# Squares of a differential head: from one full-precision pass to rounded highs and GpSimd-made lows

## What is computed

```
def rms_norm_2(x, g, eps=1e-6):
    xf = x.astype(jnp.float32)
    y = xf * lax.rsqrt(jnp.mean(xf * xf, axis=-1, keepdims=True) + eps)
    return (y * g.astype(jnp.float32)).astype(x.dtype)
...
    q = rms_norm_2(q.reshape(B, S, H, 2, d), qn_g)
    k = rms_norm_2(k.reshape(B, S, H, 2, d), kn_g)
...
        s = jnp.einsum("bhmqd,bhmkd->bhmqk", qblk, kt).astype(jnp.float32) * scale
...
        p = jax.nn.softmax(s, axis=-1)
        a = (p[:, :, 0] - lam * p[:, :, 1]).astype(vt.dtype)
        return jnp.einsum("bhqk,bhkd->bhqd", a, vt)
```

## Time and profile before

| | |
|---|---|
| median of 3 runs | 1231.56 us (1230.41 to 1232.27) |
| profiled execution | 1229.82 us, of which the span is 1228.0 us |
| PE busy | 1184.8 us, 96% |
| DVE busy | 857.9 us, 70% |
| ACT busy | 598.2 us, 49% |
| POOL busy | 62.1 us, 5% |

### The profile page before, as it was taken

How to read it: one execution, slowest core, us unless ns; L and a number is a source line. 1 busy time by engine, 2 the same in 40 slices (tenths; PEclk the granted TensorE clock), 3 DMA queues, 4 the chain that set the end, 5 groups by cost and what they waited for, 6 DMA issues and landing times.

```text
span 1228.0 us, 17185 instructions
## 1 busy us (share of the span) xinstructions
PE 1184.8 (96%) x6515; PEld 992.4 (81%) x6530; DVE 857.9 (70%) x1423; ACT 598.2 (49%) x1075; POOL 62.1 (5%) x62
## 2 busy tenths in 40 slices
PE   5999899998899999999999999999999999999998
PEld 5899788886789897777777777888887888788898
DVE  5886666758858335788888895699777687763351
ACT  6644364535546446665676655322655323652230
POOL 3029200000000000000000000000000000000001
PEclk9999999999999999999999999999999999999999
DMA  9956221110155421222212223332221432323221
GB/s 360 376 207 210 86 68 54 52 52 18 35 173 169 158 85 37 84 72 86 69 36 86 69 69 138 103 103 86 86 71 57 148 102 75 112 89 102 85 88 52
DMA packets 34002, 129.19 MB, mean 105 GB/s; under 512 B 3968, under 2 KB 4224, under 8 KB 33408
## 3 DMA queue, kind: packets, MB, share of 16 engines
q1 hardware_dynamic: 30384, 110.64, 27.5%
q0 software_dynamic: 3248, 17.14, 3.8%
q10 hardware_dynamic: 288, 0.31, 0.1%
HBM read 121.78 MB, written 6.29 MB: 104 GB/s over the span
## 4 chain that ended last, share of the span: by engine, by line
PE 64%; DVE 6%; ACT 3%; issue 2%; POOL 0%; DVEq 0%; ACTq 0%
PE bank L443 20%; PE bank L445 19%; PE bank L444 19%; PE bank L509 2%; PE bank L766 1%; DVE wl L1695 1%; DVE ca L2129 1%; PE bank L638 1%; PE bank L768 1%; DVE stat L2170 0%; DVE cumt L2378 0%; DVE ptl L1884 0%; ACT L1078 0%; ACT wh L1052 0%; PE bank L629 0%
## 5 line engine op out<-in xcount | busy, mean ns | idle before, releaser
L443 PE MATMUL bank<-hl,wh 128*128 128x512 f32 x880 | 360.9, 410 | 1.3 <-DVE cumt L1846 0.7
L445 PE MATMUL bank<-hh,wh 128*128 128x512 f32 x880 | 344.9, 392 | 0.0
L444 PE MATMUL bank<-hh,wl 128*128 128x512 f32 x880 | 344.0, 391 | 0.0
L1052 ACT ACTIVATE wh<-raw 128x1024 fp32r<-128x1024 f32 x185 | 191.2, 1055 | 192.5 <-PE bank L445 178.1
L1695 DVE TENSOR_TENSOR wl<-raw,wh 128x1024 fp32r<-128x1024 f32 x185 | 224.1, 1235 | 83.9 <-ACT wh L1052 83.4
L443 PEld LDWEIGHTS bank<-hl,wh 128*128 128x128 f32 x880 | 166.0, 189 | 38.3 <-issue 8.8
L445 PEld LDWEIGHTS bank<-hh,wh 128*128 128x128 f32 x880 | 165.7, 188 | 36.3
L444 PEld LDWEIGHTS bank<-hh,wl 128*128 128x128 f32 x880 | 166.3, 189 | 34.3 <-issue 4.3
L2129 DVE SCALAR_TENSOR_TENSOR ca<-u,vt,ca 128x512 f32<-128x512 f32 x232 | 157.7, 745 | 0.0
L443 PE MATMUL bank<-wl,hh 128*128 128x256 f32 (+1 forms) x352 | 100.5, 285 | 1.7 <-DVE cumt L1784 1.0
L444 PE MATMUL bank<-wh,hl 128*128 128x256 f32 (+1 forms) x352 | 99.3, 282 | 0.0
(11 more groups left out here) (316 smaller groups left out, 1851.7 us busy)
## 6 DMA issues: line engine op xcount, KB each, us to landing
raw<-in_chunks SPq DMA_DIRECT2D x193, 512.0 KB, 3.7
ada_a<-in_chunks SPq DMA_DIRECT2D x8, 512.0 KB, 12.8
ada_b<-in_chunks SPq DMA_DIRECT2D x8, 512.0 KB, 12.8
x<-in_x POOLq DMA_DIRECT2D x4, 512.0 KB, 10.8
mem_scratch<-kvm POOLq DMA_DIRECT2D x1, 2048.0 KB, 9.0
x<-in_x POOLq DMA_DIRECT2D x1, 2048.0 KB, 8.1
x_scratch<-x POOLq DMA_DIRECT2D x1, 2048.0 KB, 6.5
kvm<-mem_scratch POOLq DMA_DIRECT2D x1, 2048.0 KB, 8.4
```

The source lines that it names most:

```text
L443: pe.matmul(o, a[0], b[1], start=start, stop=False, **kw)
L444: pe.matmul(o, a[1], b[0], start=False, stop=False, **kw)
L445: return pe.matmul(o, a[0], b[0], start=False, stop=stop, **kw)
L1052: act.activation(wh[:, SLOT[nxt]], raw[:, RAW_SLOT[nxt]], ACT.Copy).then_inc(s.w_hi, 1)
```

## The change

For the 14 sums of the loop, ScalarE's square is written rounded, as float32r, into a new tile `sqs[:, i, 0, :]`. GpSimd then multiplies `qf` by itself in full precision into `norms[:, i, :]`, and subtracts the rounded square from it into `sqs[:, i, 1, :]`, rounded too. It waits for its own multiplication by a semaphore. TensorE sums the two parts by two rounded 512-column matmuls with `blocks_r`, a rounded copy of the block pattern that GpSimd makes once. At tt = 1 the sum now stands behind the transpose of `diff_turn`, at tt = 2 ahead of it as before. Both new tiles lie in space that other tiles of the same group leave free.

```diff
+        cos, sin, gzb, rot, sel, x, xT, kd, sqs, y = shared(...
+            [("kd", [P, 2, 2, S], F32R), ("sqs", [P, 2, 2, S], F32R)],
...
+            def head_squares(j, i):
+                pe.wait_ge(s.pattern, 1)
+                pe.wait_ge(s.sq_lo, 2 * j + i + 1)
+                total(("dns", 2 * j + 2 + i), [sqs[:, i, 0, :], sqs[:, i, 1, :]], blocks_r)
+
             for j in range(8):
...
                     diff_scores(j, tt)
-                    if tt in (1, 2) and j < 7:
-                        pe.wait_ge(s.squared, 4 + 2 + 2 * j + tt)
-                        total(("dns", 2 * j + 1 + tt), [norms[:, tt - 1, :]], blocks)
+                    if tt == 2 and j < 7:
+                        head_squares(j, 1)
                     if tt in (1, 2):
                         diff_turn(4 * j + tt - 1)
+                    if tt == 1 and j < 7:
+                        head_squares(j, 0)
                     pieces(fill, at + half, 2)
...
             pool.dma_start(x1_scratch, x[:]).then_inc(s.x1_out, 16)
+            pool.wait_ge(s.tables_in, 16 * 5)
+            pool.tensor_copy(blocks_r[:], blocks[:]).then_inc(s.pattern, 1)
+            for n in range(14):
+                i = n % 2
+                pool.wait_ge(s.sq_hi, n + 1)
+                pool.tensor_tensor(norms[:, i, :], qf[:, i, :], qf[:, i, :], ALU.mult).then_inc(s.sq_full, 1)
+                pool.wait_ge(s.sq_full, n + 1)
+                pool.tensor_tensor(sqs[:, i, 1, :], norms[:, i, :], sqs[:, i, 0, :].bitcast(F32), ALU.subtract).then_inc(s.sq_lo, 1)
             pool.wait_ge(s.v_lo, 13)
...
                         banks.wait_empty(act, key)
-                        square_q(tt)
+                        act.activation(sqs[:, tt, 0, :], qf[:, tt, :], ACT.Square).then_inc(s.sq_hi, 1)
```

More of the change, by code:

```diff
@@ L148 @@
     "qn_done": "queries and keys normalised", "of_copied": "squares of a differential head's output",
+    "pattern": "block pattern rounded", "sq_hi": "squares of queries and keys: hi", "sq_full": "whole, by GpSimd", "sq_lo": "lo",
     "x1_done": "tiles of block 1's result", "conv_done": "chunks convolved", "ln_centred": "chunks less their mean",
@@ L345, in build @@
             [("u", [P, C, PAD + S], F32)])
-        cos, sin, gzb, rot, sel, x, xT, kd, y = shared([("cos", [P, S], F32), ("sin", [P, S], F32), ("gzb", [P, 4, S], F32),
+        cos, sin, gzb, rot, sel, x, xT, kd, sqs, y = shared([("cos", [P, S], F32), ("sin", [P, S], F32), ("gzb", [P, 4, S], F32),
                                                ("rot", [P, P], F32), ("sel", [P, 8, P], BF16)],
                                               [("x", [P, T, D], F32)],
-                                              [("xT", [P, C, S], F32)], [("kd", [P, 2, 2, S], F32R)],
+                                              [("xT", [P, C, S], F32)], [("kd", [P, 2, 2, S], F32R), ("sqs", [P, 2, 2, S], F32R)],
                                               [("y", [P, C, S], F32)])
@@ L354, in build @@
         ident_b = sb("ident_b", [P, P], BF16)
-        dist, slopes, blocks, xk = shared([("dist", [P, S], F16), ("slopes", [P, 8, P], F16), ("blocks", [P, P], F32)],
+        dist, slopes, blocks, blocks_r, xk = shared([("dist", [P, S], F16), ("slopes", [P, 8, P], F16), ("blocks", [P, P], F32),
+                                                     ("blocks_r", [P, P], F32R)],
                                           [("xk", [P, 2, 2, MEM], F32R)])
@@ L830, in xq_sums @@
             def xq_sums(h):
-                pe.wait_ge(s.squared, 4 + 16 + h + 1)
+                pe.wait_ge(s.squared, 4 + 2 + h + 1)
                 total(("xns", h), [norms[:, 0, :], norms[:, 1, :]], ones)
```

## The result

The changed kernel takes 1240.27 us (1240.01 to 1240.60, 4 runs) against 1231.2 us for the one before (4 runs): 9.1 us more, a ratio of 1.0073 with a 95% interval of 1.0056 to 1.0091. Forecast was 1243.2 (1230 to 1257), slower with a chance of 0.8. The direction, the range and roughly the size held. The way to them held only in part, as the experiments show, so that the number came this near is partly luck.

The account below looks back on a forecast made before the run. TensorE was taken to bound the kernel; +2.2 at the first query, +10.2 over six periods, -0.9 and +0.2 at the end gave +11.7 on 1229.8, 1241.5, and 1243.2 with the median 1.7 higher; range 1230 to 1257.

Parts of the forecast that it names:

- TensorE saves 0.45 per sum: In the loop's 14 sums, two rounded matmuls take 0.46 us in place of 0.91, saving 6.3 us at most.
- X = 4.2 us, from additions at 1.30 to 3.58: Delay from ScalarE's square's end to TensorE's sum, through two GpSimd instructions: 4.2 us in heads 1 to 6, 3.6 at j = 0.
- Slack of 2.75 and 4.26: Time in a steady head between the square's end and TensorE's sum: 2.75 us for the query, 4.26 for the key.
- The wait adds up in a loop and sets the period: TensorE's wait at the query's sum delays the next square equally, so it recurs; each of six periods grows 1.7 us.
- VectorE's delay d is 0.7 and goes to the next square's slack: GpSimd holds VectorE up ahead of the row maximum of tt = 2, adding 0.7 us to each period.
- The key's wait at j = 0: First head's key sum: slack put at 1.72 us, X at 3.6; the sum of terms has no wait for it.
- The sum, +11.7: First query's wait +2.2, six periods +10.2, last shorter sums -0.9, key's wait +0.2: +11.7 us on the profiled execution.
- Rival: a held-up engine waits for a whole instruction: GpSimd and VectorE each block the other for a whole instruction: X 5.3, +25 us, 1256.7; chance 0.20 with beyond.
- What would make the prediction wrong: A pair under 3.2 us, a next square not moving with TensorE's wait, or VectorE's chain setting the period.
- a pair that takes under 3.2 us together: Sign against the prediction: GpSimd's multiplication and subtraction for one square together last less than 3.2 us.

Follow-up runs that it names:

- two highs: Changed kernel without GpSimd's loop; TensorE sums the rounded square twice, the low left out: 1226.8 against 1231.8 us for the kernel before, ratio 0.9957.
- two highs with the pair beside: Rounded square summed twice, while GpSimd's multiplication and subtraction run beside without TensorE waiting for them: 1238.1 us, ratio 1.0050 to the kernel before.
- fewer taps: Changed kernel with 18 convolution taps moved out of the loop into the memory attention's part: 1254.2 us, ratio 1.0189 to the kernel before.
- later sum: Changed kernel with the query's sum behind two more filling pieces and ScalarE's mean behind the exponentials of tt = 1: 1256.8 us, ratio 1.0214 to the kernel before.

## Why the prediction was right, and where it wasn't

- *TensorE saves 0.45 per sum.* Right, 0.41 measured (two highs).
- *X = 4.2 us, from additions at 1.30 to 3.58.* Too large: 3.15 in head 0, 3.4 to 3.6 in four others, and in the two in which TensorE didn't wait the low was there 2.5 us behind the square. Undisturbed, the product of a tile with itself takes 1.04 us and the rounded subtraction 1.26; disturbed, either takes up to 2.1. An instruction of 3.58 us as in the earlier trace rows came in none of the loops.
- *Slack of 2.75 and 4.26.* Right. The wait at the query's sum is there, 0.55 to 0.7 us in four of six heads, and none at the key's behind head 0.
- *The wait adds up in a loop and sets the period.* This step failed for this kernel. With the wait taken away (two highs with the pair beside) the period stays at 38.8 us, against 39.0. Such a loop may still exist, as the waits with fewer taps and X at 4.47 suggest, but here another was tighter.
- *VectorE's delay d is 0.7 and goes to the next square's slack.* This is the mis-sized term and the unseen wait. I counted only the key's pair (1.9 us less 0.94 of idle). GpSimd takes 2.9 us per head from VectorE, from both pairs, and VectorE's room in a head was 2.0 (10.2 / 5). And the delay reaches TensorE not at the next sum but earlier, at the bank that the gate's tanh frees. On ScalarE the tanh stands behind the roots, the wait for VectorE's normalising and the highs of key and query. In the kernel before, that tanh ended at 595.59 and the chunk's first matmul started at 596.20, so there was 0.6 us to spare, less the 0.41 by which the key's sum ahead of it got shorter. I had read the slack of the sums only, not of each wait that hangs on the roots.

```profile
595.01 0.58 ACT L1099 ACTIVATE th<-bank 128x512 f32<-128x512 f32 x1
...
596.20 0.39 PE L443 MATMUL bank<-hl,wh 128*128 128x512 f32 x1
```

- *The key's wait at j = 0.* It isn't in the sum, although X was put at 3.6 there and the slack at 1.72. It was 1.26 us.
- *The sum, +11.7.* Measured +9.1. The errors offset, and that is luck. The wait at a query's sum was put at 1.45 us and was 0.55 to 0.7, or nothing. What GpSimd takes from VectorE was put at 1.9 us per head and was 2.9. A period grew by 1.1 us (38.96 against 37.89) and not by 1.7, and this 1.1 is not the sum of a wait and a delay: a period is as long as VectorE's loop, 1.9 us longer than TensorE's own 37.1, and without any wait at the sums it is still 1.7 longer. Where TensorE waits at the sum, it waits less at the gate's bank (4.7 us in the five heads, against 6.3 with two highs and the pair beside).
- *Rival: a held-up engine waits for a whole instruction.* The Trainium skill's rule in SBUF — State Buffer, "Who interferes with whom", was weighed as a rival of 1256.7. Its mechanism is what the traces show. Its price was less, since in the rows read here an instruction waited at most for the rest of one instruction of the other engine. In the kernel with two highs and the pair beside, one head reads, GpSimd and VectorE:

```profile
620.29 1.04 POOL L1013 TENSOR_TENSOR sqs<-qf 128x512 fp32r<-128x512 f32 x1 [6.77 <-ACT sqs L1516]
620.34 2.07 DVE L1711 TENSOR_TENSOR wl<-raw,wh 128x1024 fp32r<-128x1024 f32 x1
621.41 2.15 POOL L1015 TENSOR_TENSOR sqs<-sqs 128x512 fp32r<-128x512 f32 x1
622.33 3.76 DVE L2145 SCALAR_TENSOR_TENSOR ca<-u,vt,ca 128x512 f32<-128x512 f32 x4
```

  GpSimd's product started first and kept its 1.04; the weight low behind it took 2.07 in place of 1.22. The subtraction then waited out the rest of the weight low (2.15 in place of 1.26), and the four taps behind took 3.76 in place of 2.73. That is the rule, seen three times in six us. What an instruction loses doesn't go by its own length. In one head of the changed kernel the pair met two small instructions of VectorE, which took 1.03 and 1.39 us, where they take 0.29 and 0.35 in the kernel before:

```profile
573.82 1.04 POOL L1013 TENSOR_TENSOR norms<-qf 128x512 f32<-128x512 f32 x1 [24.78 <-ACT sqs L1516]
573.91 1.03 DVE L2208 TENSOR_SCALAR prob<-prob,stat 128x128 f32<-128x128 f32 x1
574.94 1.28 POOL L1015 TENSOR_TENSOR sqs<-norms,sqs 128x512 fp32r<-128x512 f32 x1
574.98 1.39 DVE L2209 SCALAR_TENSOR_TENSOR prob<-prob,stat 128x128 f32<-128x128 f32 x1
```

- *What would make the prediction wrong* named the true case: that VectorE's chain and not the sum sets the period. It had no price. Another sign of it, a pair that takes under 3.2 us together, came at three of the seven queries (2.97 us at head 0, 2.40 in two heads); the other four took 3.2 to 3.4.

## What to carry to other kernels

Before work goes to GpSimd beside a busy VectorE, count what it takes from VectorE: here 2.9 us per head for 4.6 us of undisturbed GpSimd work (10 products at 1.04 and 10 subtractions at 1.26 over five heads are 23 us). For the two subtractions alone GpSimd took 1.6 us of VectorE's time per head, while VectorE does them itself in 1.0. An engine at 86% has little room if a part of the rest is a wait inside its own chain: add its work, that wait and its gaps per period, and compare the sum with the bound's period, before looking at single slacks. Then look for each wait that hangs on the same chain, banks included, since the tightest one decides and not the one that the change adds.

## What the hardware showed beyond that

Behind waits of TensorE of 1.7 to 3.1 us, which two kernels brought about, the granted clock fell in some heads, so that such a wait cost more than its length. In the kernel with the later sum, matmuls behind a wait of 3.10 us start 0.43 us apart and not 0.23, and their record is longer; the window from 533 to 543 us has a granted clock of 0.83, so a part of it at the lower of the two levels, 1.2 GHz:

```profile
533.00:543.00 10.00, 6.89 (x35) 5.43 (x34) 8.79 (x13) 1.60 (x5) 2.14 (x1) 0.83 0.50 159
```

```profile
539.51 0.77 PE L445 MATMUL bank<-ptl,vv 128*128 128x512 f32 x1 [3.10 <-ACT norms L1087]
540.08 0.63 PE L446 MATMUL bank<-pth,vv 128*128 128x512 f32 x1
540.51 0.63 PE L447 MATMUL bank<-pth,vv 128*128 128x512 f32 x1
```

The changed kernel, with waits of 0.6 to 1.6 us, stayed at 1.00 in its five heads. In the kernel with fewer taps the fall came in some heads behind waits of 1.7 us and not in others (0.94 and 0.89 in the windows from 533 to 553, 1.00 in those from 573 to 593), so no length of a wait that decides can be read from it.
